# Attention probabilities turned by DMA in 16-bit planes instead of by TensorE, and a new order of the opening

## What is computed

```python
for l in range(DEPTH):
    x = x + 0.5 * swiglu(rms_norm(x, norm_ffn1[l]), w_ffn1_in[l], w_ffn1_out[l])
    x = x + hybrid_mixer(rms_norm(x, norm_mix[l]), mem, positions, ...)
    x = x + 0.5 * swiglu(rms_norm(x, norm_ffn2[l]), w_ffn2_in[l], w_ffn2_out[l])
```

```python
p = jax.nn.softmax(logits, axis=-1).astype(v.dtype)
return jnp.einsum('bhqk,bhkd->bhqd', p, v)
```

## Time and profile before

| | |
|---|---|
| median of three runs | 1356.21 us (1355.87 to 1356.46) |
| the profiled execution | 1356.03 us, span 1354.1 |
| PE busy | 1347.8 us, 100% of the span |
| PE weight loads busy | 1141.1 us, 84% |
| DVE busy | 1031.2 us, 76% |
| ACT busy | 745.8 us, 55% |
| POOL busy | 19.5 us, 1% |
| granted TensorE clock | 1.000 of full speed |
| DMA | 248.48 MB, mean 184 GB/s |

### The profile page before, as it was taken

The page is one execution under the profiler, slowest core; times in us unless marked ns, Lnnn a source line. Parts: engine busy times, 40 slices in busy tenths (PEclk is TensorE's granted clock), DMA queues, the critical chain, the costliest instruction groups (busy, mean ns, idle before and its releaser), DMA issues.

```text
span 1354.1 us, 18963 instructions
## 1 busy us (share of the span) xinstructions
PE 1347.8 (100%) x6948; PEld 1141.1 (84%) x6948; DVE 1031.2 (76%) x1656; ACT 745.8 (55%) x1246; POOL 19.5 (1%) x48
## 2 busy tenths in 40 slices
PE   9999999999999999999999999999999999999999
PEld 7888888888888888888888888888888888888887
DVE  7888777778887678886498884786888776788853
ACT  6665455554645456664365654655546544566642
POOL 0000210000000000000000000000000000000000
PEclk9999999999999999999999999999999999999999
DMA  9566565556444546556545556545554545365561
GB/s 278 190 227 204 176 224 184 188 167 217 161 156 156 187 136 207 186 186 217 187 156 193 193 192 201 194 156 169 187 188 157 186 156 187 125 210 192 189 216 62
DMA packets 164921, 248.48 MB, mean 184 GB/s; under 512 B 10720, under 2 KB 104432, under 8 KB 164848
## 3 DMA queue, kind: packets, MB, share of 16 engines
q1 hardware_dynamic: 163664, 244.27, 54.6%
q0 software_dynamic: 896, 3.16, 0.8%
q10 hardware_dynamic: 288, 0.07, 0.0%
HBM read 245.37 MB, written 1.06 MB: 182 GB/s over the span
## 4 chain that ended last, share of the span: by engine, by line
PE 98%; DMA 1%; SPq 1%; DVE 0%; ACT 0%; issue 0%; DVEq 0%
PE psum L607 23%; PE psum L912 23%; PE psum L675 21%; PE psum L609 12%; PE psum L917 11%; PE psum L870 1%; PE psum L768 1%; PE psum L786 1%; PE psum L756 1%; DMA raw<-in_w_ffn_in 1%; PE psum L807 1%; PE psum L874 1%; PE psum L773 1%; PE psum L817 1%; PE psum L575 0%; SPq L464 0%
## 5 line engine op out<-in xcount | busy, mean ns | idle before, releaser
L1304 DVE TENSOR_TENSOR ring_lo<-raw,ring_hi 128x1024 fp32r<-128x1024 f32 x458 | 555.8, 1224 | 222.6 <-ACT ring_hi L977 217.4
L977 ACT ACTIVATE ring_hi<-raw 128x1024 fp32r<-128x1024 f32 x462 | 478.6, 1043 | 338.0 <-PE psum L917 213.1
L607 PE MATMUL psum<-hT,ring_hi 128*128 128x512 f32 x1408 | 338.3, 391 | 1.6 <-DVE small L1388 1.6
L607 PEld LDWEIGHTS psum<-hT,ring_hi 128*128 128x128 f32 x1408 | 258.1, 188 | 52.8 <-DVE small L1388 2.0
L912 PE MATMUL psum<-ring_hi,hT 128*128 128x512 f32 x960 | 241.7, 394 | 0.0
L912 PEld LDWEIGHTS psum<-ring_hi,hT 128*128 128x128 f32 x960 | 177.7, 188 | 37.9 <-issue 0.7
L609 PEld LDWEIGHTS psum<-hT,ring_lo 128*128 128x128 f32 x1408 | 180.7, 191 | 6.9
L609 PE MATMUL psum<-hT,ring_lo 128*128 128x256 f32 x1408 | 183.6, 283 | 0.0
L917 PE MATMUL psum<-ring_lo,hT 128*128 128x512 f32 x480 | 128.4, 389 | 0.0
L675 PE MATMUL psum<-ring_hi,act_hi 128*128 128x512 f32 x352 | 110.5, 389 | 0.0
L675 PE MATMUL psum<-ring_hi,act_lo 128*128 128x512 f32 x352 | 110.3, 389 | 0.0
(11 more groups left out here) (196 smaller groups left out, 1161.4 us busy)
## 6 DMA issues: line engine op xcount, KB each, us to landing
raw<-in_w_ffn_in SPq DMA_DIRECT2D x86, 1024.0 KB, 5.1
raw<-in_w_in SPq DMA_DIRECT2D x64, 1024.0 KB, 5.1
raw<-in_w_ffn_out SPq DMA_DIRECT2D x44, 1024.0 KB, 4.9
raw<-in_w_branch SPq DMA_DIRECT2D x16, 1024.0 KB, 5.2
raw<-in_w_mem_kv SPq DMA_DIRECT2D x8, 1024.0 KB, 5.1
raw<-in_w_out SPq DMA_DIRECT2D x8, 1024.0 KB, 4.9
forget<-negc_rows POOLq DMA_DIRECT2D x2, 1024.0 KB, 10.8
x<-in_x SPq DMA_DIRECT2D x4, 256.0 KB, 4.2
```

What stands on the lines that cost most here:

```text
L607: mm = pe.matmul(out[:, :], w[:, kc, :], hT_both[:, kc, :, :], start=kc == 0, stop=False)
L977: act.activation(unit_out(0, step, k), view, ACT.Copy).then_inc(hi_done.sem, 1)
L1304: dve.tensor_tensor(unit_out(1, step, k), view, unit_out(0, step, k).bitcast(F32), ALU.subtract)\
```

## The change

Four of the six groups (BY_DMA = 0, 1, 2, 4) are no longer turned by PE. For them POOL copies the low and the high halves of the probabilities into two planes in pT's own buffer, once the products before have read pT; SP issues a DMA transposition into a new buffer, planes_T, behind the loads of ka's first step (group 0), of gate(3,0)'s second (group 1), of vc's first (group 2) and of y(2,0) (group 4); POOL merges the two turned planes into pT. Their values stages move later: group 0 from the end of gate(1,1)'s first step to the middle of its second, group 1 from the end of ka's second step to the end of qc's first, group 2 from the end of kc's first step to the end of gate(3,1)'s first, group 4 from the end of gate(0,1)'s first to the end of y(0,1). Groups 3 and 5 stay as they were. POOL issues the DMAs of the forget rows after the turnings of groups 0 and 1. PE waits in scores for maxima and exponentials of the group before, in values for the split of the group before, and for groups 2 and 4 for the maxima of the group two further. DVE's maxima and ACT's exponentials of a group, which overwrite probabilities, wait for the planes of the one before.

In the first layer's opening, ACT and DVE get an order of their own for chunks 0 and 1: DVE sums chunk 0 before it computes the roots, scale and products come after both chunks' sums; PE spreads the roots between the two units of chunk 2's rounded products.

```diff
+BY_DMA, BY_PE = (0, 1, 2, 4), (3, 5)
+TURNED_BEHIND = dict(zip([_step_of("ka"), _step_of("gate", (3, 0), 1), _step_of("vc"), _step_of("y", (2, 0))], BY_DMA))
 for g, scores, exps, turned, summed in [
-    (0, _step_of("y", (1, 0)), _step_of("qa"), _step_of("qa", None, 1), _step_of("gate", (1, 1))),
-    (1, _step_of("gate", (1, 1), 1), _step_of("y", (1, 1)), _step_of("ka"), _step_of("ka", None, 1)),
-    (2, _step_of("gate", (3, 0)), _step_of("gate", (3, 0), 1), _step_of("y", (3, 0)), _step_of("kc")),
+    (0, _step_of("y", (1, 0)), _step_of("qa"), None, _step_of("gate", (1, 1), 1)),
+    (1, _step_of("gate", (1, 1), 1), _step_of("y", (1, 1)), None, _step_of("qc")),
+    (2, _step_of("gate", (3, 0)), _step_of("gate", (3, 0), 1), None, _step_of("gate", (3, 1))),
     (3, _step_of("kc", None, 1), _step_of("gate", (3, 1)), _step_of("gate", (3, 1), 1), _step_of("y", (3, 1))),
-    (4, _step_of("gate", (0, 0)), _step_of("gate", (0, 0), 1), _step_of("y", (0, 0)), _step_of("gate", (0, 1))),
+    (4, _step_of("gate", (0, 0)), _step_of("gate", (0, 0), 1), None, _step_of("y", (0, 1))),
     (5, _step_of("gate", (0, 1), 1), _step_of("y", (0, 1)), _step_of("gate", (2, 0)), _step_of("gate", (2, 0), 1)),
 ]:
...
-    _plan("values", g, summed, pe=MIDDLE if g == 5 else END, act=START if g == 5 else EARLY, dve=START if g == 5 else EARLY)
+    _plan("values", g, summed, pe=MIDDLE if g in (0, 5) else END, act={2: MIDDLE, 4: MIDDLE, 5: START}.get(g, EARLY),
+          dve={1: EARLY, 3: EARLY, 5: START}.get(g, MIDDLE))
...
                     load(L, m, dst, src)
+                    if m in TURNED_BEHIND:
+                        g = TURNED_BEHIND[m]
+                        sp.wait_ge(planes_ready.sem, planes_ready.at(L, BY_DMA.index(g) + 1))
+                        sp.dma_start_transpose(planes_T[:, 0:2 * plane_words(g)].rearrange("p (b s) -> p b s", s=P),
+                                               planes_of(g)).then_inc(planes_turned.sem, 16)
...
+                            if opening and (c, k) == (2, 0):
+                                spread_roots(L, which)
...
+                    if arg in (2, 3, 4):
+                        attended(L, 2 if arg == 3 else arg)
                     if arg:
-                        attended(L, arg)
+                        pe.wait_ge(max_ready.sem, max_ready.at(L, arg))
+                        pe.wait_ge(exp_done.sem, exp_done.at(L, arg))
...
                 elif stage == "values":
                     br, buf, c0 = heads(L, arg)
-                    pe.wait_ge(pT_act.sem, pT_act.at(L, arg + 1))
-                    pe.wait_ge(pT_dve.sem, pT_dve.at(L, arg + 1))
+                    if arg in BY_DMA:
+                        pe.wait_ge(pT_merged.sem, pT_merged.at(L, BY_DMA.index(arg) + 1))
+                    else:
+                        pe.wait_ge(pT_act.sem, pT_act.at(L, BY_PE.index(arg) + 1))
+                        pe.wait_ge(pT_dve.sem, pT_dve.at(L, BY_PE.index(arg) + 1))
+                    if arg:
+                        attended(L, arg)
+                    if arg in (2, 4):
+                        pe.wait_ge(max_ready.sem, max_ready.at(L, arg + 2))
...
+            def turned(L, g):
+
+                n, i = plane_words(g), BY_DMA.index(g)
+                planes = planes_of(g).rearrange("p (h c) -> p h c", h=2)
+                if g:
+                    pool.wait_ge(pv_ready.sem, pv_ready.at(L, g))
+                elif L:
+                    pool.wait_ge(pv_ready.sem, pv_ready.at(L - 1, 6))
+                pool.wait_ge(probs_ready.sem, probs_ready.at(L, g + 1))
+                for h in range(2):
+                    last = pool.tensor_copy(planes[:, h, :], halves_of(probs[:, 0:n])[:, h, :])
+                last.then_inc(planes_ready.sem, 1)
+                pool.wait_ge(planes_turned.sem, planes_turned.at(L, 16 * (i + 1)))
+                for h in range(2):
+                    last = pool.tensor_copy(halves_of(pT_flat[:, 0:n])[:, h, :], planes_T[:, h * n:(h + 1) * n])
+                last.then_inc(pT_merged.sem, 1)
+
             for L in range(DEPTH):
+                turned(L, 0)
+                turned(L, 1)
                 pool.wait_ge(negc_ready.sem, negc_ready.at(L, 1))
...
+                turned(L, 2)
+                turned(L, 4)
...
+                sums(0)
+                roots(0, 0)
+                lo(0, 2, 0)
+                lo(0, 2, 1)
+                sums(1)
+                lo(0, 3, 0)
+                dve.wait_ge(roots_ready.sem, roots_ready.at(0, 1))
+                scale(0)
+                scale(1)
+                product(0)
+                lo(0, 3, 1)
+                remainder(0)
+                product(1)
+                remainder(1)
...
             lo(0, 1, 1)
-            roots(0, 0)
```

More of the change, by code:

```diff
@@ L403, in first_bank, with steps_in_loop @@
             return bank[4 + kc % 4][:, at:at + SEQ]
-        def steps_in_loop(engine, body):
-            for c in range(6):
+        def steps_in_loop(engine, body, opening=None):
+            if opening is not None:
+                opening()
+            for c in range(0 if opening is None else 2, 6):
                 body(None, c)
@@ L648, in body @@
                     else:
+                        opening = (L, which) == (0, 0)
                         for k in range(2):
@@ L1016, in memory_hi, with hidden_opening, take, gate_of @@
                         last.then_inc(memh_hi.sem, 1)
+            def hidden_opening():
+                def take(c):
+                    for k in range(2):
+                        act.wait_ge(used.sem, used.at(0, 2 * c + k + 1))
+                        act.activation(small[:, c, k, :], bank[2 * c + k][:, SEQ:2 * SEQ], ACT.Copy).then_inc(small_done.sem, 1)
+                def gate_of(c):
+                    act.wait_ge(scaled.sem, scaled.at(0, 2 * c + 1))
+                    act.activation(silu[:, c, :], small[:, c, 0, :], ACT.Silu).then_inc(silu_done.sem, 1)
+                def rounded(c):
+                    act.wait_ge(prod_done.sem, prod_done.at(0, c + 1))
+                    act.activation(act_hi[:, c, :], prod[:, c, :], ACT.Copy).then_inc(act_hi_done.sem, 1)
+                take(0)
+                hi(0, 2, 0)
+                hi(0, 2, 1)
+                take(1)
+                hi(0, 3, 0)
+                act.wait_ge(roots_ps.sem, roots_ps.at(0, 1))
+                act.activation(roots_of[:, :], bank[4][:, 0:SEQ], ACT.Copy).then_inc(roots_ready.sem, 1)
+                gate_of(0)
+                hi(0, 3, 1)
+                rounded(0)
+                gate_of(1)
+                rounded(1)
             def hidden(L, base, first_chunk):
@@ L1079, in feed_forward @@
             def feed_forward(L, which, base):
-                steps_in_loop(act, hidden(L, base, which * FC))
+                steps_in_loop(act, hidden(L, base, which * FC), hidden_opening if (L, which) == (0, 0) else None)
                 for r in range(FC // 2 - 2):
@@ L1141, in task @@
                         if arg:
-                            act.wait_ge(pT_ps.sem, pT_ps.at(L, arg))
+                            act.wait_ge(planes_ready.sem, planes_ready.at(L, arg))
                         for i in range(2):
@@ L1478, in feed_forward @@
             def feed_forward(L, which, base):
-                steps_in_loop(dve, hidden(L, base, which * FC))
+                steps_in_loop(dve, hidden(L, base, which * FC), hidden_opening if (L, which) == (0, 0) else None)
                 for r in range(FC // 2 - 2):
@@ L1541, in task @@
                     if arg // 2 != MEM:
+                        if arg - 1 in BY_DMA:
+                            dve.wait_ge(planes_ready.sem, planes_ready.at(L, BY_DMA.index(arg - 1) + 1))
+                        else:
+                            dve.wait_ge(pT_ps.sem, pT_ps.at(L, BY_PE.index(arg - 1) + 1))
                         if arg // 2 == MOBA:
@@ L1575, in task @@
                 elif stage == "probsT":
-                    dve.wait_ge(pT_ps.sem, pT_ps.at(L, arg + 1))
-                    for b in range(1 if arg // 2 == MEM else 2):
+                    dve.wait_ge(pT_ps.sem, pT_ps.at(L, BY_PE.index(arg) + 1))
+                    for b in range(2):
                         last = dve.tensor_copy(pT[:, 1 + b, :], bank[5 + b][:, :])
```

76 lines of the change are left out of this document (48 added, 28 removed).

## The result

The changed kernel takes 1358.39 us (median of 20 runs) against 1356.45 for the kernel before beside it (20 runs): a ratio of 1.0014 with a 95% interval of 1.0008 to 1.0020. It is a little slower, where 0.4% faster was forecast, and 0.4 us above the range's 1358. One of the 20 runs, at 1908.89 with a mean granted clock of 0.654, was disturbed throughout and counts in no ratio.

A forecast was written before the change was run, and what follows sets the result against it. TensorE (PE), holding 98% of the chain, was taken to bound the kernel; -9.1 - 1.7 + 5.4 = -5.4 us took 1356.03 to 1350.6. The 8-in-10 range was 1344 to 1358, the forecast's own 1347.5 to 1353.5.

The forecast's parts named there:

- Transpositions off PE, -9.1: Mixer groups 0, 1, 2, 4: PE saves 4.54 us per layer, 9.1 for both, all of it counting.
- rival D: Mixer: the removed transpositions were hidden anyway; excluded because PE has no gap there, with no chance of its own given.
- The opening, -1.7: First layer's opening: chunk 0's sums no longer behind the roots, chunk 4 at 31.25 instead of 32.98, 1.7 us gained.
- Waits for the merged planes, +5.4: PE before the products of groups 0 and 2: waits of 0.9 and 1.8 us, 2.7 per layer, 5.4 in all.
- B: Rival: copies contested as in the memory's turning, waits 1.8 + 3.5 per layer, 10.6 in all, 1355.8 us; chance 0.20.
- load + 7.5 or + 8.7: Landing of a DMA transposition after the load's issue: 5.1 us plus 2.4 for memory groups or 3.6 for the others.
- a transposition as fast as a weight load: The skill's rule, not adopted: groups 0 and 2 land about 1.1 and 1.7 us earlier and their waits vanish.
- served behind the load: SP's queue: the transposition is served after the load issued before it, which lands after 5.1 us.
- 217 GB/s: Rate of the DMA transposition once it runs: 2.4 us for 0.52 MB, 3.6 for 0.79 MB.
- The edits at nothing: PE's added waits, moved products, SP's held loads and other engines' changed orders: claimed to cost nothing.
- The moved products cost what they cost: Products of the turned groups on PE, moved to later steps: claimed to add nothing to the time.
- C: Rival: POOL meets a DVE remainder at every copy, waits 7.9 us per layer, slower at 1361.0 us; chance 0.12.

The follow-up runs named there:

- experiment 1: Kernel before with only the opening's new order of ACT and DVE and spread roots, probabilities' road as it was: 1354.77 us, ratio 0.9990.
- experiments 3: Changed kernel with group 2 turned by PE again at its old steps, groups 0, 1 and 4 by DMA: 1353.28 us, ratio 0.9979 to the kernel before.
- 8: The three together, plus gate and product of chunk 1 earlier in the opening: 1348.31 us, ratio 0.9935 to the kernel before.
- experiment 4: Changed kernel with group 2's DMA transposition one load earlier, behind y(3,1)'s load instead of vc's: 1352.32 us, ratio 0.9972 to the kernel before.
- experiment 6: Changed kernel with ACT doing the gate's tanh ahead of two roundings in gate(3,0)'s second step: 1359.83 us, ratio 1.0024 to the kernel before.
- experiment 5: Changed kernel with DVE splitting group 1's products at the step's start, ahead of two remainders: 1355.43 us, ratio 0.9994 to the kernel before.
- two edits: Changed kernel with group 1's split first (experiment 5, 1355.43 us), and with group 2's transposition one load earlier (experiment 4, 1352.32 us), each alone.
- a third: Changed kernel with the gate's tanh ahead of two roundings on ACT (experiment 6): 1359.83 us.
- the three together: Changed kernel with earlier group 2 transposition, group 1's split first and the gate's tanh first: 1348.15 us, ratio 0.9943 to the kernel before.

## Why the prediction was wrong, step by step

**Transpositions off PE, -9.1: right as a size, wrong as a reason.** The half steps did shrink to 2.72. But "PE is never idle there, so all of it counts" took the instructions to be all that time was: group 2's also covered ACT's late tanh, and 0.78 per layer came back as a stop. The earlier trace rows and the earlier trace rows, by which rival D was excluded, can't show this; ACT's queue in the kernel before, with its tanh ending at 349.60, could have.

**The opening, -1.7: right.** 1.6 in the profile of experiment 1, 1.2 in the medians.

**Waits for the merged planes, +5.4: right in the sum (5.4 in the stops of the profile), less so in the parts.** Group 0 (0.4 and 0.2, where 0.9 was taken) had contested plane copies, 3.95 for both, but uncontested merging, 2.60 for both; in the profiles of experiments 3, 6 and 8 its merging took about 0.5 longer, and PE stood 0.97. Group 2 was as contested as in B: load at 356.68 where 356.5 was worked out, landing 365.39 where 365.2, merging in 5.55. PE found it 2.3 and 2.5 us late and not B's 3.5 because it came late itself, held by the two other stops: experiment 6 took one of them away and the wait grew by its size. That the sum came out is in part luck. The landing, load + 7.5 or + 8.7, was right within 0.2 in four of the profile's eight turnings (7.36 and 7.42 for group 0, 8.71 and 8.87 for groups 2 and 4 in the first layer) and 0.8 to 1.6 too early in the others (9.05 and 8.31 for group 1, 9.83 and 9.49 for groups 2 and 4 in the second layer). None of the eight came earlier by more than 0.2 (experiment 4's did, by 0.6), so a transposition as fast as a weight load, which would land 1.1 or 1.7 earlier, is not what was seen; the two terms "served behind the load" and "217 GB/s" are not shown one by one. Groups 1 and 4, taken at 0, cost 0.2 once and nothing.

**The edits at nothing: this step failed.** "The moved products cost what they cost" looked at the waits that the change adds. The one that cost 1.62 per layer is an old one, in another stage, which the moved products came too close to; experiment 5 shows it. The rest of this part held where it bears on PE. SP was held longer by an issue, 4.3 to 4.5 and 5.9 to 6.3 us where 2.5 and 3.7 were worked out, yet no load came late for PE in the mixers. (The maxima that PE waits for in the products of groups 2 and 4 are those of the next group, as the prediction has it, and not of "the group two further".)

**Not in the sum at all:** the clock behind group 2's stop, 1.6 per fall, with a fall in 16 of 19 executions of the kernel after.

Put together: -9.1 - 1.6 + 5.4 + 3.2 + 1.6 + 1.6 = +1.1, where the medians say +1.9. About 0.5 of the rest can be named: the 0.21 before group 1's products, and the eight products of a memory group taking 1.64 instead of 1.54 in three of four places. The last 0.3 stays open. Of the rivals none was right. C had the sign, but by 7.9 us of waits per layer for the merged planes, where 2.7 were found. B's no change within 0.2% is what the ratio of 1.0014 comes to, and its 10.6 us of waits are near the 10.3 that all four stops cost; but that is chance, since half of them are other waits than B's.

## What to carry to other kernels

When work moves to a later step, list every old wait on its result, in all stages, and not only those that the diff writes. When work is taken off the engine that bounds the kernel, look at what other engines finish during it: it may have been their cover. And removing a wait gains time only if the next thing that PE waits for moves earlier with it; otherwise the time goes into the next wait. Here two edits gave 3 and 6 us alone, a third cost 1.4 alone, and the three together gave 10.

## What the hardware showed beyond what was expected

- The granted clock fell to half behind a stop of PE of 2.26 us, and stayed up behind one of 2.42 in the same execution; such a fall cost 1.63. In kernels whose profile has no stop over 1.5 us in the mixer the mean was below 1.000 in 3 of 82 executions, in those with stops of 2.2 and more in 40 of 47.
- Plane copies on POOL hold up DVE's remainders too, and not only the other way round: with two of them beside it, four remainders took 7.17 instead of 4.62.
- The same transposition of 0.79 MB landed 8.0 to 10.0 us after its issue when a load had been issued 0.41 before it (24 cases in eight profiles), and 6.6 to 9.0 when 1.33 before (six cases in three). It held SP's queue for 5.1 to 7.3 us, where the load of 1 MB took 0.37.
